# A recurrent layer's first gates, decays and scans placed between its last input tiles

## The reference

```
gate, u = split(h @ w_in)                      # two halves of 1408
u = conv1d(u, width 4, causal) + conv_b
r   = sigmoid(blocks(u) @ w_a + b_a)
i_g = sigmoid(blocks(u) @ w_x + b_x)
log_a = -8 * softplus(-lam) * r;  a = exp(log_a)
b = sqrt(-expm1(2 * log_a)) * (i_g * u)
hs[t] = a[t] * hs[t-1] + b[t]                  # the scan
y = (hs * gelu(gate)) @ w_out;  x = x + g1 * y
```

## Time and profile before

| | us |
|---|---|
| median of 3 runs (lowest to highest) | 1775.16 (1775.09 to 1776.17) |
| the profiled execution, its own time | 1770.06 |
| its span on the core | 1768.2 |
| PE busy in the span | 1478.6 (84%) |
| DVE busy | 819.4 (46%) |
| ACT busy | 591.1 (33%) |

### The profile page before, as it was taken

The page is one execution under the profiler, slowest core; times in us unless marked ns, Lnnn a source line. Parts: engine busy times, 40 slices in busy tenths (PEclk is TensorE's granted clock), DMA queues, the critical chain, the costliest instruction groups (busy, mean ns, idle before and its releaser), DMA issues. The chain is left out here.

```text
span 1768.2 us, 27040 instructions
## 1 busy us (share of the span) xinstructions
PE 1478.6 (84%) x11250; PEld 1157.5 (65%) x11250; DVE 819.4 (46%) x1360; ACT 591.1 (33%) x848; POOL 33.6 (2%) x40
## 2 busy tenths in 40 slices
PE   6899998889966565565665698989999999899999
PEld 3788975568952121121121598548999998799999
DVE  5352346466641010001010567455777466877763
ACT  4331125475321000001010433364443355844332
POOL 2000020000000000000000000000000000200000
PEclk8999999999968887777687899799999999999999
DMA  9664456642729999999999663682455544344540
GB/s 398 245 230 175 166 214 230 231 159 96 281 100 388 427 427 428 428 427 428 427 428 427 258 215 119 238 332 89 168 180 186 191 168 167 119 167 181 179 166 24
DMA packets 46750, 437.95 MB, mean 248 GB/s; under 512 B 5200, under 2 KB 5456, under 8 KB 6064
## 3 DMA queue, kind: packets, MB, share of 16 engines
q1 hardware_dynamic: 45792, 430.99, 62.0%
q0 software_dynamic: 560, 5.01, 0.7%
q10 hardware_dynamic: 288, 0.32, 0.1%
HBM read 435.25 MB, written 1.05 MB: 247 GB/s over the span
## 5 line engine op out<-in xcount | busy, mean ns | idle before, releaser
L721 PE MATMUL bank<-arena_r,ring_r 128*128 128x256 f32 (+1 forms) x5416 | 724.6, 287 | 41.2 <-DVE ring_r L1758 28.1
L721 PEld LDWEIGHTS bank<-arena_r,ring_r 128*128 128x128 f32 x5416 | 693.3, 193 | 58.2 <-issue 29.2
L1758 DVE TENSOR_TENSOR ring_r<-ring,ring_r 128x2048 fp32r<-128x2048 f32 x136 | 319.0, 2349 | 246.2 <-ACT ring_r L1421 245.8
L1421 ACT ACTIVATE ring_r<-ring 128x2048 fp32r<-128x2048 f32 x136 | 259.1, 1906 | 205.1 <-PE bank L721 160.2
L1090 PE MATMUL bank<-ring,arena 128*32 128x512 f32 x1024 | 169.5, 797 | 129.1 <-DMA ring<-in_w 127.2
L1090 PEld LDWEIGHTS bank<-ring,arena 128*32 128x32 f32 x1024 | 34.2, 128 | 252.0 <-DMA ring<-in_w 147.4
L721 PE MATMUL bank<-H_r,ring_r 128*128 128x256 f32 x848 | 186.3, 293 | 4.6 <-DVE H_r L1735 4.6
L721 PEld LDWEIGHTS bank<-H_r,ring_r 128*128 128x128 f32 x848 | 142.6, 200 | 8.1 <-issue 7.6
L2019 DVE TENSOR_TENSOR arena<-arena,bank 64x512 f32<-64x512 f32 x16 | 11.1, 692 | 281.5 <-ACT arena L1523 281.5
L1523 ACT ACTIVATE arena<-bank 64x512 f32<-64x512 f32 x16 | 9.4, 588 | 368.2 <-PE bank L1090 368.2
L1117 PE MATMUL bank<-ring,arena 128*32 128x256 f32 x1024 | 86.9, 500 | 24.1 <-DMA ring<-in_w 18.8
(11 more groups left out here) (259 smaller groups left out, 1284.3 us busy)
## 6 DMA issues: line engine op xcount, KB each, us to landing
ring<-in_w SPq DMA_DIRECT2D x216, 1024.0 KB, 4.9
ring<-in_w SPq DMA_DIRECT2D x96, 2048.0 KB, 25.7
ring<-in_bias POOLq DMA_DIRECT2D x1, 2048.0 KB, 10.7
consts<-in_consts POOLq DMA_DIRECT2D x1, 1439.0 KB, 10.1
X<-in_x SPq DMA_DIRECT2D x1, 1024.0 KB, 5.3
arena<-in_ctx SPq DMA_DIRECT2D x1, 1024.0 KB, 7.8
arena<-in_decay POOLq DMA_DIRECT2D x1, 1024.0 KB, 12.2
out_t<-X SPq DMA_DIRECT2D x4, 256.0 KB, 2.0
```

Of the source, the lines that this page charges most:

```text
L721: i = nc.tensor.matmul(o, lhsT, rhs, start=start, stop=stop, skip_group_check=grouped)
L1421: f(r(hi), lo, ACT.Copy).then_inc(hi_ready, 1)
L1758: v.tensor_tensor(r(lo), lo, r(hi), ALU.subtract).then_inc(lo_ready, 1)
```

## The change

The gates are done in groups of 3, 4 and 4 tiles, the scans in groups of 2, 4 and 5. What was `rnn_decay` on DVE is now a step of its own, `rnn_square`, and the square roots on ACT are `rnn_root`. The first group's steps stand between the input tiles 5 to 10. The gated input `inp` and the scratch `rnn_d` move to the memory of `H`, which is free here, since the input product still reads the memory in which they were. The count of used gate chunks is taken at each chunk's 16th block.

```diff
-RNN_GROUPS = [range(0, 4), range(4, 8), range(8, RNN_T)]
+RNN_GROUPS = [range(0, 3), range(3, 7), range(7, RNN_T)]
+SCAN_GROUPS = [range(0, 2), range(2, 6), range(6, RNN_T)]
...
-    s += [("rnn_in", i) for i in range(RNN_T)] + [("rnn_end",)]
-    for g, tiles in enumerate(RNN_GROUPS):
-        s += [("rnn_gate", i) for i in tiles] + [("rnn_decay", g)]
-
-        s += [("rnn_out", 0)] if g == len(RNN_GROUPS) - 1 else []
-        s.append(("rnn_scan", g))
+    def gates_of(g):
+        return [("rnn_gate", i) for i in RNN_GROUPS[g]]
+
+    s += [("rnn_in", i) for i in range(6)] + gates_of(0)
+    s += [("rnn_in", 6), ("rnn_decay", 0), ("rnn_in", 7), ("rnn_square", 0), ("rnn_in", 8), ("rnn_root", 0)]
+    s += [("rnn_in", 9), ("rnn_scan", 0), ("rnn_in", 10), ("rnn_end",)] + gates_of(1)
+    s += [("rnn_decay", 1), ("rnn_square", 1)]
+    s += gates_of(2) + [("rnn_root", 1), ("rnn_out", 0), ("rnn_decay", 2), ("rnn_scan", 1), ("rnn_square", 2)]
+    s += [("rnn_root", 2), ("rnn_scan", 2)]
     s += [("rnn_out", j) for j in range(1, (RNN_T + 1) // 2)]
...
-        rec, inp = room(8481, RNN_T, T), room(11297, RNN_T, T)
-        thr, rnn_d = room(2816, RNN_T, T), room(14113, 2, T)
+        rec, thr = room(8481, RNN_T, T), room(2816, RNN_T, T)
+        inp = h_flat[:, 0:RNN_T * T].rearrange("p (a b) -> p a b", a=RNN_T)
+        rnn_d = h_flat[:, RNN_T * T:RNN_T * T + 2 * T].rearrange("p (a b) -> p a b", a=2)
...
-                    if i // 16 != seen[0]:
-                        if seen[0] >= 0:
-                            owed[0] += 1
-                        seen[0] = i // 16
...
-                if n == RNN_T - 1:
-                    owed[0] += 1
+                    if i % 16 == 15 or i == len(GATE_TILES) - 1:
+                        owed[0] += 1
...
-            def step_rnn_scan(g):
+            def step_rnn_root(g):
                 for i in RNN_GROUPS[g]:
                     act.wait_ge(rnn_sqrt_in, i + 1)
...
-            def step_rnn_decay(g):
+            def step_rnn_square(g):
...
             def step_rnn_scan(g):
-                for i in RNN_GROUPS[g]:
+                for i in SCAN_GROUPS[g]:
```

More of the change, by code:

```diff
@@ L1290, in step_rnn_in @@
                     xa_tiles(("rnn_in", i))
-            seen = [-1]
             def step_rnn_gate(n):
@@ L1642, in _ @@
                      "nsa_s": step_nsa_s, "nsa_t": step_nsa_t, "ffn_in": step_ffn_in, "rnn_in": step_rnn_in,
-                     "rnn_gate": step_rnn_gate, "rnn_decay": step_rnn_decay, "rnn_scan": step_rnn_scan,
+                     "rnn_gate": step_rnn_gate, "rnn_decay": step_rnn_decay, "rnn_root": step_rnn_root,
                      "lift": step_lift, "root": step_root}
@@ L2228, in _ @@
                      "nsa_o": step_nsa_o, "nsa_out": step_nsa_out, "ffn_in": step_ffn_in, "ffn_add": step_ffn_add,
-                     "rnn_in": step_rnn_in, "rnn_decay": step_rnn_decay, "rnn_scan": step_rnn_scan,
+                     "rnn_in": step_rnn_in, "rnn_square": step_rnn_square, "rnn_scan": step_rnn_scan,
                      "rnn_add": step_rnn_add}
```

## The result

| | before | after |
|---|---|---|
| median, us (lowest to highest) | 1775.62 (1773.87 to 1780.2), 7 runs | 1790.6 (1785.68 to 1795.46), 7 runs |
| the profiled execution, its own time | 1770.06 | 1794.57 |
| its span | 1768.2 | 1792.6 |
| PE, DVE, ACT busy | 1478.6, 819.4, 591.1 | 1489.2, 816.4, 595.4 |

The changed kernel is slower: ratio 1.0084 (95% interval 1.0066 to 1.0103), which is +15.0 us. The forecast was 1793.7 in a range of 1785 to 1799.

What follows compares the result with a forecast made beforehand. The input phase was taken as bound by a closed chain of DVE and ACT, the stretch behind it by DVE. 16.5 - 0.5 + 2.5 = +18.5 us on 1775.16 gave 1793.7 us, range 1785 to 1799.

Steps and rivals of the forecast that it cites:

- The closed chain, 16.5 us: Input tiles 5 to 10: work added to the DVE-ACT chain lengthens the period one for one, last scaling +16.5 us.
- The rival in which the moved work hides: Input phase: ACT's and DVE's idle is true slack, so faster, 1765.8 us; 5 in 100.
- tanh behind gelu needs no load: Decay 0 on ACT, between input tiles: no table load taken for tanh after gelu; otherwise +1.3 us.
- A switch at twice its row: Rival, input phase: six more switches each cost another 1.28 us, about 7 us more, 1801 us; 3 in 100.
- Behind the input tiles, -0.5 us: Last scaling to the end of rnn_out 3's remainder: 50.9 us against 51.4, with gates 5 and 6 2.0 us longer.
- DVE's new wait: Tail: DVE stands 7.5 us at rnn_out 2's remainder, its split being behind gates 7 to 10 and root 1.
- The rival without that wait: Tail: ACT reaches rnn_out 2's split while DVE still has squares, up to 7.5 us back, 1786.2 us; 8 in 100.
- The clock, +2.5 us: Last three output products: a lower PE clock after the wait for DVE costs +2.5 us, nothing if the clock holds.
- The rival in which the clock holds: Neither gates 5 and 6 nor rnn_out 3 run at half speed: +14.0 us, 1789.2 us; 20 in 100.
- 5.1 us were carried over: Whole launch: timed median taken as 5.1 us above the profiled execution, as before, turning 1788.6 into 1793.7 us.
- The 1.79 us before 1503.53 cost no speed: Kernel before, behind the input tiles: a PE wait of 1.79 us was read as leaving the clock unslowed.
- the 2.7 of the working: Behind the last input tile: PE was to have waited 2.7 us before gate 3.

Runs made afterwards that it cites:

- the two places of the same loads: Kernel before plus four pairs of ACT table loads, ahead of the next split (1786.95 us) or behind it (1772.0 us); before beside them 1771.76 us.
- With the chain open: DVE's remainder moved behind the input tile's scaling: in the kernel before 1772.21 us, timed again 1768.74 (ratio 0.997); in the changed kernel 1775.59.
- the filling kernel: Changed kernel plus 48 matmuls whose result nobody reads, between rnn_out 2 and rnn_out 3: 1789.26 us, before beside it 1774.58.
- the last kernel: Changed kernel with remainders behind scalings, gates 0 to 2 in banks 4 to 6, later steps reordered, rnn_out 1 ahead of square 2: 1762.06 us, ratio 0.9937.

## Why the prediction was right

**The closed chain, 16.5 us.** Shown. The five intervals were forecast at 11.24, 11.6, 7.8, 8.7 and 9.1 and measured at 11.36, 11.62, 7.79, 8.71 and 9.05, and the two places of the same loads (+12.04 against none) show the rule behind them. With the chain open the change cost 8.9 us instead of 17.7. The rival in which the moved work hides falls with it. That tanh behind gelu needs no load was right: the phase has the loads that were counted.

**A switch at twice its row.** Falls: the loads are 1.28 us each and a pair costs 3.01 us in the chain. The page counts 851 ACT instructions after against 848, the three loads more.

**Behind the input tiles, -0.5 us.** Measured -0.8. The first square comes 11.5 us behind the last scaling (11.6 foreseen), and DVE's new wait is 7.30 (7.5 foreseen). Its cause is the pair of orders that the working names, the split behind gates 7 to 10 and root 1, and the scans behind the remainder: the kernel that moves root 1 and scan 1 together gets 6.75 back. Neither was moved alone. The rival without that wait falls.

**The clock, +2.5 us.** The right mechanism, sized too high: 16.48 - 14.64 = 1.84 us. The term was taken from 48 matmuls of the earlier trace rows that lost 2.5; those had the clock at 0.50 for 5.4 us of work (1545.87 to 1551.2), after's for 4.2 us (1577.50 to 1581.7). Gates 5 to 10 took 16.63 us for 68 records, the first of them at 0.50; at the rate of the earlier trace rows that would be 15.0, so 1.6 where 2.0 were counted. The rival in which the clock holds falls.

**The sum.** 16.7 - 0.8 + 1.8 is the stage's +17.7 against +18.5. The medians differ by 15.0, with an interval of 11.7 to 18.3. The stage lies toward the interval's upper end, and the forecast of +18.5 just outside it. Why is open. The timed runs have no stage length, but the filling kernel repeats the changed one's to its last scaling (90.58 against 90.56 us), so it is more likely the rest of the launch that differs. The step from profiled to timed did not hold: before's profiled execution is below its median, and 5.1 us were carried over for that, where after's is 4.0 above.

**What did not hold.** "The 1.79 us before 1503.53 cost no speed" was true of that row and not as a rule. After, PE waits 1.80 us at 1509.15 before the matmuls of input tile 10, and the windows from 1510 to 1513 show 0.50: 7.51 us instead of 6.01. DVE hid it. It is also why PE waits 1.15 us before gate 3 and not the 2.7 of the working, which had tile 10's matmuls at full clock. The filling kernel's 1.82 us did the same on the path that sets the end.

## What to carry to other kernels

Idle time on an engine with an in-order queue is slack only at the place in its queue where nothing behind it is awaited by the chain; the same loads cost 3.0 us a period ahead of the split and nothing behind it. So before moving work into idle time, write down who waits for the next instruction of that engine, and first open the chain: here that one move was worth 5.4 us alone and 14.3 in the changed kernel. The rest of the new order has a price of its own: on the open chain the change as it stood still cost 8.9 us. Judge edits of this size by the length of the stage, since single launches of one kernel differed by up to 12 us.

## Unexpected of the hardware

Waits of nearly one length had different effects on the clock. The 1.79 us of the earlier trace rows were followed by 104 records at full speed, and the 1.85 us of the last kernel by 48 more. But 1.80 us at 1509.15 in the changed kernel (after waits of 1.53 and 1.20 us in the 27 us ahead of it) and 1.82 us in the filling kernel (after 19.9 us of work, and a wait of 6.58 ahead of that) were each followed by 3.4 us at 0.50. In both, the fall came some 0.8 us after PE had begun to work again. The kernel with the loads ahead of the split has two waits of nearly one length in a row, of which the first cost nothing:

```profile
1489.99 5.98 PE L721 MATMUL bank<-arena_r,ring_r 128*128 128x258 f32 x48 [3.37 <-DVE arena L2156]
1499.38 8.63 PE L721 MATMUL bank<-arena_r,ring_r 128*128 128x258 f32 x48 [3.40 <-DVE arena L2156]
```

The clock stayed at 1.00 through the first and fell at 1498.5, within the second. What decides between them these runs don't settle.
